# Down projection of a gated hybrid layer: statistics by schedule, evictions with the norm weight, residual adds on VectorE

## The reference, cut to what matters

```
def rmsnorm(x, g):
    r = lax.rsqrt(jnp.mean(xf * xf, axis=-1, keepdims=True) + EPS)
    return xf * r * g
h = rmsnorm(x, g_pre_mix)               # statistics of the next tokens feed this
p = h @ w_in                            # 1024 -> 6144
...
h2 = rmsnorm(x, g_pre_mlp)
f = jnp.square(jax.nn.relu(h2 @ w_up)) @ w_down     # 4096 -> 1024
x = x + rmsnorm(f, g_post_mlp)
```

## Time and profile before

| what | value |
|---|---|
| median of 3 runs | 1077.98 us (1076.97 to 1162.92) |
| the profiled execution | 1077.83 us, span on the slowest core 1076.8 us |
| spans of the eight cores | 1073.3 to 1076.8 us |
| TensorE matmul busy | 989.5 us, 92% of the span |
| VectorE, ScalarE, GpSimd busy | 518.3, 309.5, 251.6 us |
| down projection of pass 0 | 404.1 to 540.4 us |
| first stage of pass 1, up to the gates | 540.4 to 673.3 us |
| last matmul | ends at 1068.6 us |

### The profile page before, as it was taken

How to read it: one execution, slowest core, us unless ns; L and a number is a source line. 1 busy time by engine, 2 the same in 40 slices (tenths; PEclk the granted TensorE clock), 3 DMA queues, 4 the chain that set the end, 5 groups by cost and what they waited for, 6 DMA issues and landing times.

```text
span 1076.8 us, 16102 instructions; the slowest of 8 cores (1073.3 to 1076.8 us)
## 1 busy us (share of the span) xinstructions
PE 989.5 (92%) x5221; PEld 487.7 (45%) x5322; DVE 518.3 (48%) x885; ACT 309.5 (29%) x631; POOL 251.6 (23%) x370
## 2 busy tenths in 40 slices
PE   2589999999799999759999999999998999999996
PEld 2444444444344444324444455555544555544443
DVE  1558764334953440342188887433388434401334
ACT  4212223224533331310122223322264333301111
POOL 4011112112521113022333332111154111121132
PEclk9889999999999999889999999999999999999999
DMA  9959999963094229625964434964404622231141
GB/s 226 175 79 131 144 117 147 122 104 50 21 138 88 79 80 177 193 80 160 150 172 68 79 53 67 218 141 71 68 1 74 99 70 67 67 117 59 40 157 79
DMA packets 46545, 113.75 MB, mean 106 GB/s; under 512 B 7040, under 2 KB 9344, under 8 KB 46208
## 3 DMA queue, kind: packets, MB, share of 16 engines
q0 software_dynamic: 38976, 86.79, 47.5%
q1 hardware_dynamic: 7344, 25.89, 7.1%
q10 hardware_dynamic: 144, 0.03, 0.0%
HBM read 164.20 MB, written 18.49 MB: 170 GB/s over the span
## 4 chain that ended last, share of the span: by engine, by line
PE 82%; DVE 8%; issue 5%; ACT 2%; DMA 2%; POOL 1%; DVEq 0%; ACTq 0%; POOLq 0%
PE PS L135 81%; DVE TM L165 3%; DVE TM L155 2%; DVE AR L155 2%; ACT TM L152 2%; DMA WS<-w_in 2%; POOL AR L155 1%; PE PS L139 1%; DVE STAT L442 0%; DVEq L220 0%; ACT STAT L152 0%; DVE TM L171 0%; DVE TM L160 0%; DVE AR L171 0%; POOL WS L126 0%
## 5 line engine op out<-in xcount | busy, mean ns | idle before, releaser
L135 PE MATMUL PS<-AR,WS 128*128 128x512 bf16 (+1 forms) x3596 | 666.4, 345 | 35.9 <-DVE AR L155 10.1
L135 PEld LDWEIGHTS PS<-AR,WS 128*128 128x128 bf16 x3664 | 330.4, 100 | 364.1 <-issue 42.5
L135 PE MATMUL PS<-WS,AR 128*128 128x512 bf16 x1331 | 299.6, 383 | 4.5 <-DVE TM L165 2.8
L152 ACT ACTIVATE TM<-PS 128x512 f32<-128x512 f32 (+3 forms) x234 | 130.4, 570 | 269.9 <-PE PS L135 269.9
L135 PEld LDWEIGHTS PS<-WS,AR 128*128 128x128 bf16 x1360 | 133.8, 99 | 162.9 <-issue 9.9
L155 DVE TENSOR_TENSOR AR<-TM 128x512 bf16<-128x512 f32 (+1 forms) x200 | 119.5, 610 | 136.1 <-ACT TM L152 132.0
L155 POOL TENSOR_TENSOR AR<-AR,TM 128x1024 f32<-128x1024 f32 (+1 forms) x34 | 66.8, 1966 | 165.6 <-DVE TM L165 153.0
L126 POOL DMA_DIRECT2D WS<-wd_bf x96 | 51.7, 540 | 196.7 <-PE PS L135 193.1
L126 POOL DMA_DIRECT2D WS<-w_in x96 | 51.5, 552 | 187.8 <-PE PS L135 172.0
L152 ACT ACTIVATE TM<-PS,CS 128x512 f32<-128x512 f32 (+1 forms) x80 | 49.7, 623 | 133.9 <-PE PS L135 113.9
L155 DVE TENSOR_TENSOR TM<-PS,TM 128x512 f32<-128x512 f32 (+1 forms) x40 | 24.4, 610 | 115.6 <-PE PS L135 115.6
(11 more groups left out here) (54 smaller groups left out, 360.8 us busy)
## 6 DMA issues: line engine op xcount, KB each, us to landing
WS<-w_in POOLq DMA_DIRECT2D x96, 256.0 KB, 6.8
WS<-wd_bf POOLq DMA_DIRECT2D x96, 256.0 KB, 3.0
WS<-w_up POOLq DMA_DIRECT2D x64, 256.0 KB, 5.5
AR<-x_p SPq DMA_DIRECT2D x16, 512.0 KB, 16.4
wd_bf<-w_dn POOLq DMA_DIRECT2D x8, 1024.0 KB, 23.1
y_p<-AR SPq DMA_DIRECT2D x16, 512.0 KB, 2.7
WS<-w_oc POOLq DMA_DIRECT2D x16, 256.0 KB, 12.2
WS<-w_o POOLq DMA_DIRECT2D x16, 256.0 KB, 14.6
```

The lines of the kernel that those rows point to most:

```text
L135: return self.add("pe", lambda e: e.matmul(out, lhsT, rhs, start=start, stop=stop), reads=[lhsT, rhs], writes=[out], signal=sig, name="mm")
L152: return self.add("act", lambda e: e.activation(out, in_, func, **kw), reads=rd, writes=wr, name=name)
```

## The change

- `steps` is now a table from unit to work. Tile i is loaded at unit 2+3i, into one of two buffers `XQ`, and squared at unit 6+3i. The broadcasts and the rescaling of `hT` are one step, `st_scale`: tiles 0 to 3 at unit 21, 4 to 7 at unit 37, tile 8 at unit 43; it takes its bank and gives it back in that step.
- First half of a group (`post0`): ScalarE squares from the bank, then VectorE multiplies the bank by the norm weight into `F0` (an added dependency puts it after the square), in place of copy and square of the copy.
- Second half (`post1`): `F0` times the factor plus the residual is one VectorE operation; the other half's add moves from GpSimd to VectorE. `Y1` is one buffer per pass, elsewhere.
- The very last tile (`last_tile`): its last half is computed in two pieces of 256 columns in two banks, 32 matmuls each; each piece is squared and multiplied by the weight on its own, and the two halves of the output row are stored separately, the last one from ScalarE's DMA queue.

```
-        XQ = tmv(0, F32, [D])
-        Y1 = [tmv(4096 + i * 2048, F32, [512]) for i in range(2)]
+        XQ = [tmv(i * 4096, F32, [D]) for i in range(2)]
+        Y1 = [tmv(16384, F32, [512]), tmv(0, F32, [512])]
...
+                def st_scale(tiles):
+                    b = banks.one()
+                    n = len(tiles) * 128
+                    a = tiles[0] * 128
+                    for c, i in enumerate(tiles):
+                        P.mm(PS[:, b, c * 128:(c + 1) * 128],
+                             bass.AP(STT_, nx_r[i][0], [[64, 128], [0, 128]]), IDF[:, :], start=True, stop=True)
+                    for k in range(KC):
+                        P.stt("dve", hT[:, k, a:a + n], hT[:, k, a:a + n], cs(C_GPM + k), PS[:, b, 0:n],
+                              ALU.mult, ALU.mult, name="hsc")
+                    banks.give(b)
+
                 for i in range(NTILE_B):
-                    steps += [at(i, st_load), None, at(i, st_sq), at(i, st_bc)]
+                    at(2 + 3 * i, st_load, i)
+                    at(6 + 3 * i, st_sq, i)
+                at(21, st_scale, (0, 1, 2, 3))
+                at(37, st_scale, (4, 5, 6, 7))
+                at(43, st_scale, (8,))
...
+                    def post0(i):
+                        pm = PS[:, bk[i], :]
+                        op, ss = square(pm, 512)
+                        times_g(F0[G.index(i)], pm, a1, op)
+                        banks.give(bk[i])
+                        P.ts("dve", ss, ss, EPS, None, ALU.add, name="ssa")
+                        ssA[i] = ss
...
+                    def post1(i):
+                        pm = PS[:, bk[i], :]
+                        _, ss = square(pm, 512)
+                        rstd(ss, ssA[i])
+                        P.stt("dve", y1, pm, ss, GBC[:, 1, a1:a1 + 512], ALU.mult, ALU.mult, name="mlpn1")
+                        banks.give(bk[i])
+                        residual(i, a0, F0[G.index(i)], ss)
+                        P.tt("dve", x1[:, i, a1:a1 + 512], x1[:, i, a1:a1 + 512], y1, ALU.add, name="y1")
+                        store(i, 0, 1024, "sp")
+
+                    def last_tile(i):
+                        b = (bk[i], banks.one())
+                        ss = ssA[i]
+                        for h in range(2):
+                            pm = PS[:, b[h], 0:256]
+                            for q in range(16):
+                                w = W.rhs(keys[q])
+                                for kk in range(2):
+                                    P.mm(pm, actT[:, q * 2 + kk, i * 128:(i + 1) * 128],
+                                         w[:, kk, h * 256:(h + 1) * 256], start=(q == 0 and kk == 0),
+                                         stop=(q == 15 and kk == 1))
+                            op, sh = square(pm, 256)
+                            if h == 0:
+                                P.tt("dve", ss, ss, sh, ALU.add, name="ssa")
+                            else:
+                                P.act(sh, sh, AF.Sqrt, bias=ss, name="sqrt")
+                            times_g(y1[:, h * 256:(h + 1) * 256], pm, a1 + h * 256, op)
+                        P.add("dve", lambda e: e.reciprocal(sh, sh), reads=[sh], writes=[sh], name="rstd")
+                        residual(i, a0, F0[G.index(i)], sh)
+                        store(i, a0, 512, "sp")
+                        residual(i, a1, y1, sh)
+                        store(i, a1, 512, "act")
+                        banks.give(*b)
```

More of the change, by code:

```diff
@@ L803, in build_program, with at @@
                 W.free((ps_i, "up", f))
-            steps = []
+            steps = {}
+            def at(unit_, f, *args):
+                steps.setdefault(unit_, []).append(lambda: f(*args))
             if not last:
@@ L810, in build_program @@
                     P.dma("pool", hT[:, :, a:a + n], xbT[:, :, a:a + n], "xbt%d" % a, name="xbT")
-                rb = {}
+                nx_r = {}
                 def st_load(i):
-                    P.dma("sp", XQ, nx_tin[i], "xq", name="xstat")
+                    P.dma("sp", XQ[i % 2], nx_tin[i], "xq%d" % (i % 2), name="xstat")
                 def st_sq(i):
[L817 to L832, removed]
@@ L834, in at @@
[L834 to L837 removed]
+                    nx_r[i] = mean_sq(JNK5, XQ[i % 2])
+                    rstd(nx_r[i][1])
+                def st_scale(tiles):
[9 more added lines that the diff above has]
+                    banks.give(b)
@@ L839, in build_program @@
+                for i in range(NTILE_B):
+                    at(2 + 3 * i, st_load, i)
[3 more added lines that the diff above has]
+                at(43, st_scale, (8,))
             unit = [0]
             def tick():
[L842 to L845, removed]
+                for f in steps.pop(unit[0], ()):
+                    f()
@@ L865, in mm2 @@
                                  signal=(kk == 1 and (sig or q == 15)))
[L867 to L888, removed]
@@ new lines, in build_program, with square, times_g @@
+                    a0, a1 = (1 - nh) * 512, nh * 512
+                    y1 = Y1[ps_i]
+                    def square(src, n):
+                        i_, ss = stat()
+                        op = P.act(JNK5[:, 0:n], src, AF.Square, scale=1.0 / 32.0, accum_out=ss, name="sq")
+                        return op, ss
+                    def times_g(out, pm, col, after):
+                        n = out.shape[-1]
+                        P.tt("dve", out, pm, GBC[:, 1, col:col + n], ALU.mult, name="fg").deps.add(after)
@@ new lines, in post0, with residual @@
+                    def post0(i):
[5 more added lines that the diff above has]
+                        ssA[i] = ss
+                    def residual(i, col, f, r, n=512):
+                        P.stt("dve", x1[:, i, col:col + n], f, r, x1[:, i, col:col + n], ALU.mult, ALU.add, name="y")
@@ new lines, in store @@
+                    def store(i, col, n, q):
+                        P.dma(q, tout[i][:, col:col + n], x1[:, i, col:col + n], "yo%d_%d" % (i, col), name="ystore",
+                              is_output=True)
+                    def post1(i):
[7 more added lines that the diff above has]
+                        store(i, 0, 1024, "sp")
@@ L890, in build_program @@
+                    post = post0 if hi == 0 else post1
                     if final:
-                        for i in G:
+                        for i in G[:-1]:
                             for q in range(16):
@@ L894, in build_program @@
                             post(i)
+                        last_tile(G[-1])
                     else:
@@ L903, in build_program @@
                             post(i)
-            while steps:
-                tick()
+            assert not steps
         P.emit(stack)
```

## The result

| | before | changed |
|---|---|---|
| median | 1077.9 us | 1047.8 us |
| ratio, 95% interval | | 0.972 [0.970, 0.974] |
| span of the profiled execution, slowest core | 1076.8 | 1045.9 |
| down projection of pass 0 | 136.3 | 112.5 |
| first stage of pass 1 | 132.9 | 128.4 |

Forecast were 1048.2 us, a range of 1043.5 to 1053.5, and faster by over 2% at 0.91. The slowest core was core 0 before and is core 6 here; the cores reach the down projection at times up to 3.5 us apart before and 3.8 here. Some executions of most kernels had cores at a lower granted clock and took longer (1163 us before, 1177 changed), so the times of the experiments are medians of the other executions, and where these are few or none, stage lengths of cores at the usual clock (0.97 to 0.99 over the whole run).

A forecast was written before the change was run, and what follows sets the result against it. TensorE, busy 92% of the span, was taken as the bound, so gains lie where it idles or runs at a lower clock. 23.8 + 3.7 + 2.1 = 29.6 off 1077.8 gives 1048.2 us, range 1043.5 to 1053.5.

The forecast's parts named there:

- Part 1: Down projection of pass 0: the new schedule removes TensorE's two waits for statistics and the clock loss behind them, 23.8 us.
- The five units of distance: Down projection of pass 0: broadcasts ask for statistics five units after the eviction round, not one.
- That the loads stand ahead of the stores: SP queue: all nine loads precede the first stores (unit 32), where tile 8's stood behind four; no time given.
- The evictions with the norm weight: First half of a group: the bank is freed later, about 1.5 us after the last matmul; costed at 0, up to 1 us.
- Part 2: Last round of pass 0 on VectorE alone: pass 1's first projection starts earlier, 3.7 us, ends 0 and 8.0.
- Until then VectorE's chain sets the pace: Pass 1's first stage until 616.08: VectorE's early start should come through to TensorE nearly whole, 3.7 us.
- Part 3: End of the kernel: last tile in two pieces with fewer operations and a smaller last store, 2.1 us, between 1.5 and 2.8.
- The bound "1.567": Round on VectorE: upper bound in us for the add, today's time beside GpSimd's add; 0.70 was expected.
- Rival 1 and 2: Pass 1's first stage: part 2 yields nothing (1051.9 us, chance 0.13) or all 8.0 (1043.9 us, chance 0.08).
- Rival 3: Pass 0's down projection: late weight loads or a late statistic cause a new stall, 6.2 plus 2.3 us; 1056.7; chance 0.07.
- Rival 4: TensorE from 404 to about 588: unbroken work lowers the granted clock to 0.76, 58 us more; 1106 us; chance 0.03.
- the limiter: Peak-current limit holding a die at 13/16 clock once three cores run dense matmuls; 184 us would be 226, time 1091.

The follow-up runs named there:

- the late squares: Changed kernel with loads at units 2+4i and squares at 4+4i as before, broadcasts still at 21, 37 and 43; 1050.7 us.
- run with GpSimd's add: Changed kernel with the add of the second half in each round moved back to GpSimd, with two Y1 buffers; one execution at 1047.0 us.

## Why the prediction was right, step by step

- **Part 1, forecast 23.8 us, measured 23.9.** The stage went from 136.4 (134.6 to 136.4 over the cores) to 112.5 (112.7 on two cores) in every run that has the squares of the new schedule. The reason given, squares behind a round, is shown by the broadcasts moved back to their old units at no cost. The five units of distance, which I named beside it, are a second cover; with the short rounds they would nearly do alone. That the loads stand ahead of the stores I had noted without a price; the late squares give one, 1.0 to 3.4 us of waiting at unit 43. The loads were earlier than bounded: tile 3's square is at 416.3, tile 8's at 448.8.
- **The evictions with the norm weight, 0.** No wait for a bank appeared; the stretch to the last matmul is 396.2 on the slowest core and 395.3 before, and the 393.6 of six others is the clock behind one wait, as told above, not the evictions.
- **Part 2, forecast 3.7, measured 4.45** (4.3 to 4.8 over the cores). The round on VectorE gave 13.4 - 8.9 = 4.5 where I had 3.8: a tile takes 2.23 us, not 2.40, since the gap after the reciprocal is there for two tiles of four only, and the add too overlaps what follows it (0.60 from start to start, not 0.70). All of it came through to TensorE, as taken. "Until then VectorE's chain sets the pace" holds at that size, not further: without a round TensorE would gain 2.2 more, not 3.6.
- **Part 3, forecast 2.1, measured 2.6** (2.4 to 2.7 over the cores). The operations took 2.70 where I had 2.83, the store 0.6 less than before where I took 0.3, the pieces 0.1 more as taken.
- **The bound "1.567" for the add** didn't matter: it takes 0.68. Before, the add ended 0.55 us after GpSimd's (543.84 and 543.29): most of its 1.57 was waiting.
- **Rival 1 and 2** (0 and 8.0 of part 2): neither. **Rival 3**, transfers: weight loads were in time, though the DMA share of the stage rose to 0.85. **Rival 4**, the clock: over 403.2 to 588 it was 0.99 to 1.00 on all eight cores, so TensorE's rest was not what kept its clock up. By the limiter that the prediction cites from the Trainium skill ("TensorE: Matmul & The Clock Gate", section "Seeing it yourself") this stretch would have been 42 us longer (226 - 184); at a granted clock of 0.99 to 1.00 it didn't act in it.

The sum: 23.9 + 4.45 + 2.6 = 30.95, the difference of the spans (30.9); what the slowest core gained before 404 (0.9) it lost again after 644. Forecast were 29.6. So parts 2 and 3 were sized 1.3 too small together, and the profiled execution, 1046.97 us, is 1.2 below the forecast. That the median came within 0.4 is luck: it is 0.8 above the profiled execution, and the slowest core is one of the two on which the clock fell in pass 1.

## What to carry to other kernels

Ask of each small operation on which the busiest engine waits what is emitted ahead of it on its own engine and its own DMA queue; here the place in these lists did more than the distance between producer and consumer. Parts that remove the same wait don't add up, so time each alone and all but one. Where a second engine lags by a fixed block of work, let the first work after it be light on that engine: reordering the blocks was worth 9.7 us more, for one line.

## What was new about the hardware

Beside a GpSimd add of two SBUF operands, VectorE's `tensor_tensor` of two SBUF operands took 1.57 us instead of 0.68 and a tiny f32 copy 1.23 instead of 0.16, but `scalar_tensor_tensor` with two SBUF operands 0.74 to 0.84 instead of 0.74. The last is not free: it began before GpSimd's add or in its last 0.3 us, and the add, which takes 1.13 us from the end of this operation on, took up to 1.71. So a slow row of one engine can be the other's doing, and the engine whose operation begins first shows no sign of it. The Trainium skill ("SBUF — State Buffer", section "SBUF: two separate sides") has a VectorE operation with two SBUF inputs and a GpSimd operation that reads SBUF take turns, the one that starts first holding the other up for its whole length. The traces agree for `tensor_tensor` (kernel before: it ends 0.55 us after GpSimd's add) and for `scalar_tensor_tensor` (run with GpSimd's add: there GpSimd waits for it). The copy has one SBUF input only; why it waited as well no run here shows.
